# The normalised input h made straight from PSUM by ScalarE and VectorE, and the first loads in another order

## The chip, the cores and the metric

The kernel runs on one core of a Trainium2 chip. The metric is the device time of one execution, in microseconds, median of several runs.

## The reference

Two layers of an encoder over 256 positions and 2048 channels, all in f32. Cut to what matters here:

```
for l in range(2):
    h    = rms_norm(x, g_mix_pre[l])
    proj = h @ w_in[l]                     # 2048 -> 4096: q, k, v, and u for the pooling
    attn = dilated_mixture_attention(rope(q), rope(k), v)
    pool = multiscale_pool(u, w_pool[l], pool_scale[l])
    x    = x + rms_norm(concat(rms_norm(attn), rms_norm(pool)) @ w_out[l], g_mix_post[l])
    h2   = rms_norm(x, g_ffn_pre[l])
    f    = square(relu(h2 @ w_up[l])) @ w_down[l]        # 2048 -> 8192 -> 2048
    x    = x + rms_norm(f, g_ffn_post[l])
```

A product of two f32 matrices is made on TensorE as three products of rounded operands: every operand v is split into a high part (v rounded to the type fp32r) and a low part (v minus the high part), and hi*hi + lo*hi + hi*lo is summed in PSUM.

## The kernel before

**Units.** The work is cut into units: 512 output columns, all 2048 input channels, both row tiles t = 0, 1 of 128 positions. The weights of a unit are 8 pairs (two tiles of 128 channels by 512 columns, 512 KB). A pair goes through SyncE's DMA into one of 4 slots of `raw`, ScalarE casts it to `w_hi` (L692), VectorE subtracts and gets `w_lo` (L964), and TensorE uses it in 6 matmuls for t = 0 and in 6 more for t = 1 (`pair`, L377 to L379). `w_hi` and `w_lo` have 8 slots each; a slot is free again after its t = 1 matmuls (`w_used`), a `raw` slot after L964 (`lo_made`). `unit` runs n = 0 to 3: n = 0, 1 are the two halves of the input channels for t = 0, n = 2, 3 the same for t = 1; p = 0 to 3 are the pairs of a half. A place in a unit is written (n, p) below.

**The chunks of h.** h is needed transposed. It is 8 chunks: i = 4t + c is row tile t, channels 512c to 512c + 511. For each, TensorE transposes four blocks of x into `t_bank[i % 2]` (`h_turns`, L405); VectorE multiplies by the norm weight, which is one number per partition and block, and copies to `xg` in SBUF (`scaled`, L971); ScalarE casts that to `h_hi` (L697); GpSimd subtracts and gets `h_lo` (`stationary_lo`, L1297). `t_bank` is free for chunk i + 2 when `xg` of chunk i is made, `xg` when `h_lo` is made. The factor 1/rms of a row comes only with the result (L727). A matmul pair of the first unit on h waits for the chunk that holds its channels.

**Transitions.** h is made four times: at the start, in the middle of each layer (before the first unit with w_up), and between the layers. In these three transitions chunks 0 and 1 are transposed two pairs ahead of chunks 2 and 3, at the end of the product before; chunks 4, 5 are transposed at (1, 1) and chunks 6, 7 at (2, 1) of the first unit on h. x itself is renewed by VectorE (`add_posts`, L991) from the sum `acc`, GpSimd's product with the norm weight (L1324), and 1/rms, which GpSimd makes (L1316) from squares that ScalarE sums (L872, L713).

**What sets the order.** All of it is written out by hand: each engine runs its own list in order, and semaphores bind the lists. What stands behind a waiting instruction on its engine waits too. Loops over layers, groups and units are real loops on every engine.

## Time and profile before

| | us |
|---|---|
| median of 3 runs | 2080.79 (2079.71 to 2081.98) |
| span of the profiled execution | 2081.2 |
| TensorE busy, and share of the span | 2046.5, 98% |
| VectorE busy, share | 1088.2, 52% |
| ScalarE busy, share | 998.6, 48% |
| GpSimd busy, share | 212.1, 10% |

The span runs from the first to the last instruction of the core; it lies 0.4 us above the median and within the runs. No other time of the profiled execution is given, so the span stands for it. The page also has the granted clock of TensorE and the DMA traffic in 40 slices of the span; over the whole span 183 GB/s were moved.

### The profile page before, as it was taken

Reading aid. Unit: us, or ns where it says so; the run is one execution under the profiler, and the core shown is the slowest. Engines: PE = TensorE matmul, PEld = TensorE weight load, DVE = VectorE, ACT = ScalarE, POOL = GpSimd, SP = SyncE. Lnnn points to the kernel's source line nnn. Section 1 sums busy time; section 2 is a strip of 40 time slices with the busy share of each in tenths; the row PEclk is TensorE's granted clock in tenths of the full one; section 3 lists DMA queues with packets and bytes.
Section 4 is the critical chain, followed back from the end, with each engine's and each line's share of the span. In section 5 each row is a group of like instructions: output and inputs, shape, how many; then the busy total and the mean of one; then the engine's idle time right before and its main releaser. Section 6 shows DMA issues by size and latency. Waiting matters only on the chain.

```text
span 2081.2 us, 28816 instructions
## 1 busy us (share of the span) xinstructions
PE 2046.5 (98%) x9298; PEld 1695.0 (81%) x9298; DVE 1088.2 (52%) x1105; ACT 998.6 (48%) x1247; POOL 212.1 (10%) x248
## 2 busy tenths in 40 slices
PE   7999999999999999999989999999999999999998
PEld 5888887888888888888878888878888888888886
DVE  6554657554554554554554446664454454454454
ACT  5444656543553453454454446565345444444542
POOL 3951014000000000000120010230000000000001
PEclk9999999999999999999999999999999999999999
DMA  6664454565565555655556544555565566466463
GB/s 214 222 207 137 140 184 160 177 205 186 181 196 188 187 189 188 213 191 182 165 195 208 191 142 130 166 185 183 185 202 191 173 202 200 162 195 230 161 196 128
DMA packets 196518, 381.65 MB, mean 183 GB/s; under 512 B 11904, under 2 KB 14048, under 8 KB 195808
## 3 DMA queue, kind: packets, MB, share of 16 engines
q1 hardware_dynamic: 195776, 379.12, 55.7%
q10 hardware_dynamic: 672, 1.61, 0.2%
q8 instruction: 42, 0.69, 0.1%
q14 instruction: 28, 0.23, 0.0%
HBM read 378.59 MB, written 2.10 MB: 183 GB/s over the span
## 4 chain that ended last, share of the span: by engine, by line
PE 48%; issue 41%; POOL 8%; DMA 1%; DVE 0%; POOLq 0%; ACT 0%; SPq 0%; ACTq 0%; DVEq 0%
PE acc_bank L377 16%; PE acc_bank L379 16%; PE acc_bank L378 16%; POOL acc L1324 2%; POOL h_lo L1297 1%; PE t_bank L637 1%; POOL f_lo L1297 1%; DMA post_row<-in_g_ffn_post 1%; DMA x<-in_x 1%; POOL rstd L1316 0%; PE t_bank L405 0%; POOL band L1453 0%; POOL band L1447 0%; POOL tmp L1417 0%; POOL tmp L1423 0%
## 5 line engine op out<-in xcount | busy, mean ns | idle before, releaser
L964 DVE TENSOR_TENSOR w_lo<-raw,w_hi 128x1024 fp32r<-128x1024 f32 x704 | 871.5, 1250 | 573.4 <-ACT w_hi L692 538.9
L692 ACT CAST w_hi<-raw 128x1024 fp32r<-128x1024 f32 x704 | 734.1, 1052 | 481.7 <-PE acc_bank L379 265.9
L377 PE MATMUL acc_bank<-w_hi,h_hi 128*128 128x512 f32 x1536 | 608.9, 396 | 3.9 <-POOL h_lo L1297 2.2
L379 PE MATMUL acc_bank<-w_hi,h_lo 128*128 128x512 f32 x1536 | 600.0, 391 | 0.0
L378 PE MATMUL acc_bank<-w_lo,h_hi 128*128 128x512 f32 x1536 | 599.3, 390 | 0.0
L377 PE MATMUL acc_bank<-w_hi,f_hi 128*128 128x512 f32 x1216 | 477.4, 393 | 0.0
L379 PE MATMUL acc_bank<-w_hi,f_lo 128*128 128x512 f32 x1216 | 473.5, 389 | 0.0
L378 PE MATMUL acc_bank<-w_lo,f_hi 128*128 128x512 f32 x1216 | 473.1, 389 | 0.0
L377 PEld LDWEIGHTS acc_bank<-w_hi,h_hi 128*128 128x128 f32 x1536 | 289.8, 189 | 65.4 <-DVE w_lo L964 4.0
L379 PEld LDWEIGHTS acc_bank<-w_hi,h_lo 128*128 128x128 f32 x1536 | 289.0, 188 | 61.3
L378 PEld LDWEIGHTS acc_bank<-w_lo,h_hi 128*128 128x128 f32 x1536 | 289.7, 189 | 57.9
L379 PEld LDWEIGHTS acc_bank<-w_hi,f_lo 128*128 128x128 f32 x1216 | 228.2, 188 | 47.9
L378 PEld LDWEIGHTS acc_bank<-w_lo,f_hi 128*128 128x128 f32 x1216 | 228.4, 188 | 46.6
L377 PEld LDWEIGHTS acc_bank<-w_hi,f_hi 128*128 128x128 f32 x1216 | 228.3, 188 | 46.3
L1324 POOL TENSOR_TENSOR acc<-acc,post_row 128x512 f32<-128x512 f32 x32 | 43.2, 1353 | 1369.0 <-ACT junk L872 1369.0
L911 ACT CAST f_hi<-t_bank 128x512 f32 x64 | 37.6, 587 | 216.7 <-PE t_bank L637 216.7
L1221 DVE TENSOR_TENSOR f_lo<-t_bank,f_hi 128x512 f32 (+1 forms) x64 | 44.3, 692 | 186.0 <-ACT f_hi L911 186.0
L902 ACT ACTIVATE act_f<-acc_bank,rstd 128x512 f32<-128x512 f32 x64 | 43.8, 685 | 99.0 <-PE acc_bank L379 99.0
L1234 DVE TENSOR_TENSOR acc<-acc_bank,acc 128x512 f32 (+1 forms) x48 | 33.0, 688 | 99.2 <-PE acc_bank L379 99.2
L872 ACT ACTIVATE junk<-acc 128x512 f32<-128x512 f32 (+1 forms) x32 | 20.2, 632 | 93.0 <-DVE acc L1234 58.2
L1297 POOL TENSOR_TENSOR h_lo<-xg,h_hi 128x512 fp32r<-128x512 f32 x32 | 55.3, 1749 | 38.6 <-ACT h_hi L697 38.6
L1297 POOL TENSOR_TENSOR f_lo<-xg,f_hi 128x512 fp32r<-128x512 f32 x16 | 20.5, 1293 | 339.8 <-ACT f_hi L697 339.8
(150 smaller groups left out, 822.2 us busy)
## 6 DMA issues: line engine op xcount, KB each, us to landing
raw<-in_w_up SPq DMA_DIRECT2D x256, 512.0 KB, 4.4
raw<-in_w_down SPq DMA_DIRECT2D x256, 512.0 KB, 5.4
raw<-in_w_in SPq DMA_DIRECT2D x128, 512.0 KB, 4.8
raw<-in_w_out SPq DMA_DIRECT2D x64, 512.0 KB, 5.3
w_pool_s<-in_w_pool SPq DMA_DIRECT2D x2, 1024.0 KB, 8.5
post_row<-in_g_mix_post SPq DMA_DIRECT2D x2, 1024.0 KB, 7.3
post_row<-in_g_ffn_post SPq DMA_DIRECT2D x2, 1024.0 KB, 7.9
out<-x SPq DMA_DIRECT2D x8, 256.0 KB, 2.7
```

Source lines behind the costliest of these rows:

```text
L377: pe.matmul(bank[:, :], xh, wh, start=begin and k == 0, stop=False)
L378: pe.matmul(bank[:, :], xh, wl, start=False, stop=False)
L379: mm = pe.matmul(bank[:, :], xl, wh, start=False, stop=end and k == 1)
L637: tr = pe.transpose(t_bank[t][:, h_cols(j)], act_f[:, t, h_cols(j)], ident[:, :])
L692: act.copy(w_hi[:, half * PAIRS + p, :], raw[:, p, :]).then_inc(hi_made, 1)
L902: act.activation(act_f[:, t, :], acc_bank[t][:, :], ACT.Relu, scale=rstd[:, COL_X2 + t:COL_X2 + t + 1]).then_inc(acc_free[t], 1)
L911: act.copy(f_out(f_hi, u, t), t_bank[t][:, :].rearrange("p (k n) -> p k n", k=4)).then_inc(fhi_made, 1)
L964: dve.tensor_tensor(w_lo[:, slot, :], raw[:, p, :], w_hi[:, slot, :].bitcast(F32), ALU.subtract).then_inc(lo_made, 1)
L1221: dve.tensor_tensor(f_out(f_lo, u, t), t_bank[t][:, :].rearrange("p (k n) -> p k n", k=4), f_out(f_hi, u, t).bitcast(F32), ALU.subtract).t ...
L1234: dve.tensor_tensor(dst, acc_bank[t][:, :], dst, ALU.add).then_inc(acc_free[t], 1)
L1297: pool.tensor_tensor(lo, xg[:, slot, :].rearrange("p (k n) -> p k n", k=k), hi.bitcast(F32), ALU.subtract).then_inc(st_lo, 1)
L1324: pool.tensor_tensor(part, part, post_row[:, c_cols(c)], ALU.mult).then_inc(post_ready, 1)
```

## The change

1. **h without a copy.** ScalarE makes `h_hi` straight from `t_bank` in PSUM: four instructions of 128x128 for a chunk, each with its norm weight as per-partition scale (`h_hi_pair`). VectorE makes `h_lo` from `t_bank`, the norm weight and `h_hi`: four instructions of 128x128 (t_bank times gain minus h_hi). L971, L697 and L1297 go for the 32 chunks of h (the y and attention chunks keep them), and GpSimd has no part in h.
2. **Waits.** VectorE waits for all of a chunk's `h_hi`. TensorE's transposes of chunk i >= 2 wait for `h_lo` of chunk i - 2, where they waited for `xg` of chunk i - 2. TensorE's matmuls wait for half chunks.
3. **First loads.** The norm weights and the second half of x's first row tile are issued first by ScalarE, without a wait; SyncE issues the first half, four weight pairs, the second row tile, the small inputs, and then goes on with weights.
4. **The start.** VectorE makes no zeros in `acc` and does not add them to x. Chunks 2 and 3 are transposed within the first unit, before (0, 1) and (0, 2), and the other norm weights before (1, 3). The lists of ScalarE and VectorE mix chunks and weight pairs in another order.

The diff, with some of the like pieces left out:

```diff
                 with sp.Fori(0, CHUNKS) as c:
                     load_unit(w_down, l, g * D, c * CH, hu + 2 * CHUNKS + c * 2)
+            load_half(w_in, 0, 0, 3 * HALF_W, 0)
+            sp.dma_start(x[:, 1, :], x_rows[1]).then_inc(x_loaded[2], 16)
+            row = 0
+            for g in (g_ffn_pre, g_attn_out, g_pool_out):
+                n = DEPTH * g.shape[1] // P
+                sp.dma_start(rows_others[row:row + n, :], g.rearrange("l (k p) -> (l k) p", p=P)
+                             ).then_inc(others_loaded, 16)
+                row += n
+            sp.dma_start(pos_i[:, :], positions[0].rearrange("(t p) -> p t", p=P),
+                         allow_slow_non_contiguous=True).then_inc(pos_loaded, 16)
             with sp.Fori(0, DEPTH) as l:
                 hu = l * HU_LAYER
-                with sp.Fori(0, 2) as u:
-                    load_unit(w_in, l, 0, 3 * HALF_W + u * CH, hu + u * 2)
+                with sp.If(l > 0):
+                    load_half(w_in, l, 0, 3 * HALF_W, hu)
+                load_half(w_in, l, HALF_W, 3 * HALF_W, hu + 1)
+                load_unit(w_in, l, 0, 3 * HALF_W + CH, hu + 2)
                 sp.wait_ge(acc_done, l * ACC_LAYER + 1)
...
                     pe.wait_ge(x_ready, l * 16 + 8 * h + i + 1)
                     if i >= 2:
-                        pe.wait_ge(xg_ready, l * XG_LAYER + (0, XG_H2)[h] + i - 1)
+                        pe.wait_ge(h_lo_made, h_pair(l, h, i - 1))
                     for j in range(4):
                         tr = pe.transpose(t_bank[i % 2][:, h_cols(j)],
                                           x[:, t, c * CH + j * P:c * CH + (j + 1) * P],
...
                         h_turns(l, h, (4, 5))
                     if (n, p) == (2, 1):
                         h_turns(l, h, (6, 7))
-                    if p % 2 == 0:
-                        pe.wait_ge(st_lo, XG_SLOTS + l * XG_LAYER + (0, XG_H2)[h]
-                                   + 2 * n + p // 2 + 1)
+                    pe.wait_ge(h_lo_made, h_pair(l, h, 2 * n + p // 2) + p % 2 + 1)
                 return before
...
                          ).then_inc(gains_turned, 1)
             h_turns(0, 0, (0, 1))
-            pe.wait_ge(others_loaded, 16 * 3)
-            pe.transpose(s_bank[1][:, 0:4 * KT], rows_others[:, :], ident[0:4 * KT, 0:4 * KT]
-                         ).then_inc(gains_turned, 1)
-            h_turns(0, 0, (2, 3))
+            def others_turn():
+                pe.wait_ge(others_loaded, 16 * 3)
+                pe.transpose(s_bank[1][:, 0:4 * KT], rows_others[:, :], ident[0:4 * KT, 0:4 * KT]
+                             ).then_inc(gains_turned, 1)
             with pe.Fori(0, DEPTH) as l:
                 hu0 = l * HU_LAYER
                 a0 = l * ACC_LAYER
                 xg0 = XG_SLOTS + l * XG_LAYER
-                unit(hu0, a0, h_hi, h_lo, h_first_unit(l, 0))
+                h_before = h_first_unit(l, 0)
+                def first_before(n, p):
+                    if (n, p) in ((0, 1), (0, 2)):
+                        with pe.If(l < 1):
+                            h_turns(0, 0, (p + 1,))
+                    if (n, p) == (1, 3):
+                        with pe.If(l < 1):
+                            others_turn()
+                    h_before(n, p)
+                unit(hu0, a0, h_hi, h_lo, first_before)
                 with pe.Fori(1, 6) as u:
                     unit(hu0 + u * 2, a0 + u, h_hi, h_lo)
...
                     act.wait_ge(w_used, hu * PAIRS + p + 1)
                     act.copy(w_hi[:, half * PAIRS + p, :], raw[:, p, :]).then_inc(hi_made, 1)
+            def h_hi_pair(bank, g, dst):
+                for n in range(2):
+                    for j in (2 * n, 2 * n + 1):
+                        hi = act.mul(dst[:, j, :], bank[:, h_cols(j)],
+                                     gain[:, g + j:g + j + 1])
+                    hi.then_inc(h_hi_made, 1)
             def stationary_hi(i, dst, slot, k):
...
             def h_chunks(l, h, which):
                 for i in which:
                     t, c = i // CHUNKS, i % CHUNKS
-                    stationary_hi(l * XG_LAYER + (0, XG_H2)[h] + i,
-                                  h_hi[:, 4 * c:4 * c + 4, h_cols(t)], i % 2, 4)
+                    act.wait_ge(tb_done[i % 2], l * TB_LAYER + (0, TB_H2)[h] + i // 2 + 1)
+                    h_hi_pair(t_bank[i % 2], (G_MIX, G_FFN)[h] + 4 * c,
+                              h_hi[:, 4 * c:4 * c + 4, h_cols(t)])
             def h_squares(l, h, t):
...
+            x_rows = x_in[0].rearrange("(t p) d -> t p d", p=P)
+            act.dma_start(rows_mix[:, :], g_mix_pre.rearrange("l (k p) -> (l k) p", p=P)
+                          ).then_inc(gains_loaded, 16)
+            act.dma_start(x[:, 0, D // 2:], x_rows[0][:, D // 2:]).then_inc(x_loaded[1], 16)
             act.wait_ge(ones_made, 1)
             act.copy(warm[:, :], ones[:, :]).then_inc(warm_done, 1)
-            x_rows = x_in[0].rearrange("(t p) d -> t p d", p=P)
-            act.wait_ge(x_loaded[0], 16)
-            row = 0
-            for g in (g_ffn_pre, g_attn_out, g_pool_out):
-                n = DEPTH * g.shape[1] // P
-                act.dma_start(rows_others[row:row + n, :], g.rearrange("l (k p) -> (l k) p", p=P)
-                              ).then_inc(others_loaded, 16)
-                row += n
-            act.dma_start(x[:, 0, D // 2:], x_rows[0][:, D // 2:]).then_inc(x_loaded[1], 16)
-            act.dma_start(pos_i[:, :], positions[0].rearrange("(t p) -> p t", p=P),
-                          allow_slow_non_contiguous=True).then_inc(pos_loaded, 16)
+            act.wait_ge(gain_ready, 1)
+            h_chunks(0, 0, (0,))
             split_hi(0, 0, (0,))
-            act.dma_start(x[:, 1, :], x_rows[1]).then_inc(x_loaded[2], 16)
-            h_chunks(0, 0, (0, 1))
-            split_hi(0, 0, (1, 2))
-            h_chunks(0, 0, (2, 3))
-            split_hi(0, 0, (3,))
+            h_chunks(0, 0, (1,))
+            split_hi(0, 0, (1, 2, 3))
+            h_chunks(0, 0, (2,))
             split_hi(1, 1, (0,))
+            h_chunks(0, 0, (3,))
             with act.Fori(0, DEPTH) as l:
                 hu0 = l * HU_LAYER
...
                 mix_square(0, 2)
                 mix_square(0, 3)
                 split_hi(hu_f, 0)
+                act.wait_ge(gain_ready, 4 + 2 * l)
                 h_chunks(l, 1, (0, 1))
...
             def h_chunks(l, h, which):
                 for i in which:
-                    dve.wait_ge(tb_done[i % 2], l * TB_LAYER + (0, TB_H2)[h] + i // 2 + 1)
-                    scaled(l * XG_LAYER + (0, XG_H2)[h] + i, i % 2, t_bank[i % 2],
-                           (G_MIX, G_FFN)[h] + 4 * (i % CHUNKS), 4)
+                    t, c = i // CHUNKS, i % CHUNKS
+                    g = (G_MIX, G_FFN)[h] + 4 * c
+                    for n in range(2):
+                        dve.wait_ge(h_hi_made, h_pair(l, h, i) + 2)
+                        for j in (2 * n, 2 * n + 1):
+                            lo = dve.scalar_tensor_tensor(
+                                h_lo[:, 4 * c + j, h_cols(t)], t_bank[i % 2][:, h_cols(j)],
+                                gain[:, g + j:g + j + 1],
+                                h_hi[:, 4 * c + j, h_cols(t)].bitcast(F32),
+                                ALU.mult, ALU.subtract)
+                        lo.then_inc(h_lo_made, 1)
...
-            def h_first_unit(l, h, hu):
-                add_posts(l, h, (4, 5))
+            def h_first_unit(l, h, hu, late=True):
+                if late:
+                    add_posts(l, h, (4, 5))
                 split_lo(hu + 1, 1, (2, 3))
...
             dve.wait_ge(x_loaded[0], 16)
             dve.sem_inc(x_ready, 2)
             dve.wait_ge(gain_ready, 1)
-            h_chunks(0, 0, (0, 1))
-            split_lo(0, 0, (0, 1))
             dve.wait_ge(x_loaded[1], 16)
             dve.sem_inc(x_ready, 2)
-            h_chunks(0, 0, (2, 3))
-            split_lo(0, 0, (2, 3))
+            h_chunks(0, 0, (0,))
+            split_lo(0, 0, (0,))
+            h_chunks(0, 0, (1,))
+            split_lo(0, 0, (1, 2, 3))
+            h_chunks(0, 0, (2,))
+            split_lo(1, 1, (0,))
+            h_chunks(0, 0, (3,))
+            split_lo(1, 1, (1,))
+            dve.wait_ge(x_loaded[2], 16)
+            dve.sem_inc(x_ready, 4)
+            h_first_unit(0, 0, 0, False)
             dve.wait_ge(gains_turned, 2)
             half = KT // 2
             for at_col, n, src in ((G_FFN, KT, 0), (G_ATTN, half, 2 * KT), (G_POOL, half, 3 * KT)):
...
                 src = s_bank[1][:, (2 + n) * KT:(3 + n) * KT]
                 dve.tensor_copy(gains_half[:, n, 0:DEPTH, :],
                                 src.rearrange("p (l k) -> p l k", l=DEPTH)).then_inc(gains_ready, 1)
-            split_lo(1, 1, (0, 1))
             dve.wait_ge(gain_ready, 4)
             dve.wait_ge(gains_ready, 4)
-            dve.wait_ge(setup_done, 4)
...
                 pool.tensor_tensor(lo, xg[:, slot, :].rearrange("p (k n) -> p k n", k=k),
                                    hi.bitcast(F32), ALU.subtract).then_inc(st_lo, 1)
-            def h_chunks(l, h, which):
-                for i in which:
-                    t, c = i // CHUNKS, i % CHUNKS
-                    stationary_lo(l * XG_LAYER + (0, XG_H2)[h] + i,
-                                  h_hi[:, 4 * c:4 * c + 4, h_cols(t)],
-                                  h_lo[:, 4 * c:4 * c + 4, h_cols(t)], i % 2, 4)
             def h_first_unit(l, h):
                 root(l, (RS_X1, RS_X2)[h], (COL_X1, COL_X2)[h])
-                h_chunks(l, h, range(4, 8))
                 root(l, (RS_X1, RS_X2)[h] + 1, (COL_X1, COL_X2)[h] + 1)
```

## Where the instructions stand

The rows name the line, the operation, output <- inputs and what is waited for. First TensorE at the start of the program, before:

```order
L430 MATMUL s_bank<-ident,rows_mix 128x32 [waits gains_loaded,ident_made]
L405 MATMUL t_bank<-ident,x 128x128 [waits x_ready]
L405 MATMUL t_bank<-ident,x 128x128 x3
L405 MATMUL t_bank<-ident,x 128x128 [waits x_ready]
L405 MATMUL t_bank<-ident,x 128x128 x3
L434 MATMUL s_bank<-ident,rows_others 128x64 [waits others_loaded]
L405 MATMUL t_bank<-ident,x 128x128 [waits xg_ready,x_ready]
L405 MATMUL t_bank<-ident,x 128x128 x3
```

And in the change, up to the first matmuls of the first pair and the transposes of chunk 2 (L420 is now the line of the transposes, L392 to L394 are the pair's):

```order
L443 MATMUL s_bank<-ident,rows_mix 128x32 [waits gains_loaded,ident_made]
L420 MATMUL t_bank<-ident,x 128x128 [waits x_ready]
L420 MATMUL t_bank<-ident,x 128x128 x3
L420 MATMUL t_bank<-ident,x 128x128 [waits x_ready]
L420 MATMUL t_bank<-ident,x 128x128 x3
...
L392 MATMUL acc_bank<-w_hi,h_hi 128x512 [waits lo_made]
L393 MATMUL acc_bank<-w_lo,h_hi 128x512
L394 MATMUL acc_bank<-w_hi,h_lo 128x512
...
L420 MATMUL t_bank<-ident,x 128x128 [waits h_lo_made,x_ready]
L420 MATMUL t_bank<-ident,x 128x128 x3
```

The product with the other norm weights and chunks 2 and 3 stood ahead of the first pair, and now stand behind or within it.

Second, VectorE in the middle of a layer, from the end of the four instructions on x, before:

```order
L991 SCALAR_TENSOR_TENSOR x<-acc,rstd,x 128x512 [waits post_ready]
...
L971 TENSOR_TENSOR xg<-t_bank,gain 128x512 [waits st_lo]
L970 REGISTER_ALU [waits tb_done1]
L971 TENSOR_TENSOR xg<-t_bank,gain 128x512 [waits st_lo]
...
L964 TENSOR_TENSOR w_lo<-raw,w_hi 128x1024 [waits hi_made]
...
L1179 SCALAR_TENSOR_TENSOR acc<-acc_bank,rstd,acc 128x512 [waits w_used]
```

And in the change (L1020 is the line on x, L1031 makes h_lo, L993 w_lo, L1223 is L1179 before):

```order
L1020 SCALAR_TENSOR_TENSOR x<-acc,rstd,x 128x512 [waits post_ready]
...
L1031 SCALAR_TENSOR_TENSOR h_lo<-t_bank,gain,h_hi 128x128 [waits h_hi_made]
L1031 SCALAR_TENSOR_TENSOR h_lo<-t_bank,gain,h_hi 128x128
...
L993 TENSOR_TENSOR w_lo<-raw,w_hi 128x1024 [waits hi_made]
...
L1223 SCALAR_TENSOR_TENSOR acc<-acc_bank,rstd,acc 128x512 [waits w_used]
```

The place in VectorE's list is the same, but what stood there waited for TensorE (`tb_done`) and GpSimd (`st_lo`), and now waits for ScalarE (`h_hi_made`).

Third, ScalarE at the same place, in the change (L716 casts w_hi, L722 makes h_hi, L899 sums squares of acc):

```order
L716 CAST w_hi<-raw 128x1024 [waits w_used]
L917 ISA
L722 ACTIVATE h_hi<-t_bank,gain 128x128 [waits tb_done0,gain_ready]
L722 ACTIVATE h_hi<-t_bank,gain 128x128 x3
L722 ACTIVATE h_hi<-t_bank,gain 128x128 [waits tb_done1]
L722 ACTIVATE h_hi<-t_bank,gain 128x128 x3
L898 REGISTER_ALU [waits acc_free1]
L899 ACTIVATE junk,ss_post<-acc 128x512 [waits sq_done]
L722 ACTIVATE h_hi<-t_bank,gain 128x128 [waits tb_done0]
```

The eight instructions of chunks 0 and 1 stand where two casts from `xg` stood: behind the last of four weight casts, and chunks 2 and 3 stay behind the squares.

## Rows read from the trace of the kernel before

**Rows 1.** The page: busy time of each engine, share of the span, instructions
```profile
PE 2046.5 (98%) x9298; PEld 1695.0 (81%) x9298; DVE 1088.2 (52%) x1105; ACT 998.6 (48%) x1247; POOL 212.1 (10%) x248
```

**Rows 2.** Waits of TensorE: us in total, times, longest
```profile
PE t_bank L405 <- DVE x L991: 10.0, 6, 4.6
```

**Rows 3.** Timeline, start: start us, us, engine, line, tiles, [idle before <-releaser]
```profile
5.87 1.97 PE L405 MATMUL t_bank<-ident,x 128*128 128x128 f32 x8 [3.03 <-DVEq L1030]
...
7.16 0.44 ACTq L748 DMA_DIRECT2D x<-in_x  x1
...
8.32 1.04 ACT L692 CAST w_hi<-raw 128x1024 fp32r<-128x1024 f32 x1 [6.02 <-DMA raw<-in_w_in]
...
13.88 1.97 PE L405 MATMUL t_bank<-ident,x 128*128 128x128 f32 x8 [1.96 <-DVEq L1035]
...
15.50 0.78 PE L377 MATMUL acc_bank<-w_hi,h_hi 128*128 128x512 f32 x1
```

**Rows 4.** DMA, the first 60 us in 40 slices of 1.5 us
```profile
GB/s 0 104 233 309 366 407 356 339 376 391 408 218 22 165 212 300 156 362 335 305 242 22 11 0 11 0 0 0 35 302 305 247 307 328 374 400 379 395 389 341
```

**Rows 5.** Timeline: end of the first unit, and the second
```profile
32.12 0.50 PE L377 MATMUL acc_bank<-w_hi,h_hi 128*128 128x512 f32 x1 [2.16 <-POOL h_lo L1297]
...
34.43 0.47 PE L377 MATMUL acc_bank<-w_hi,h_hi 128*128 128x512 f32 x1
...
39.67 3.88 ACT L692 CAST w_hi<-raw 128x1024 fp32r<-128x1024 f32 x4
...
54.36 0.50 PE L377 MATMUL acc_bank<-w_hi,h_hi 128*128 128x512 f32 x1 [0.20 <-DVE w_lo L964]
```

**Rows 6.** Timeline of the first mid-layer transition, TensorE, ScalarE, VectorE
```profile
317.23 3.48 DVE L964 TENSOR_TENSOR w_lo<-raw,w_hi 128x1024 fp32r<-128x1024 f32 x3
...
317.87 1.14 ACT L697 CAST h_hi<-xg 128x512 fp32r<-128x512 f32 x2
...
318.08 1.03 PE L405 MATMUL t_bank<-ident,x 128*128 128x128 f32 x8
...
330.71 2.32 DVE L991 SCALAR_TENSOR_TENSOR x<-acc,rstd,x 128x512 f32<-128x512 f32 x2 [0.54 <-POOL rstd L1316]
...
332.43 1.97 PE L405 MATMUL t_bank<-ident,x 128*128 128x128 f32 x8 [2.40 <-DVE x L991]
...
334.05 0.78 PE L377 MATMUL acc_bank<-w_hi,h_hi 128*128 128x512 f32 x1
```

**Rows 7.** Windows around it: us, busy time of each engine, granted clock (PEclk), DMA
```profile
331.00:336.00 5.00, 3.57 (x13) 3.21 (x14) 5.00 (x8) 2.43 (x8) 1.36 (x2) 0.66 0.50 146
```

**Rows 8.** Timeline of the transition between the layers, ScalarE and TensorE
```profile
1037.24 1.05 ACT L692 CAST w_hi<-raw 128x1024 fp32r<-128x1024 f32 x1 [1.82 <-PE acc_bank L379]
...
1046.70 0.63 ACT L872 ACTIVATE junk<-acc 128x512 f32<-128x512 f32 x1 [0.94 <-DVE acc L1234]
...
1050.95 2.94 ACT L692 CAST w_hi<-raw 128x1024 fp32r<-128x1024 f32 x3 [3.53 <-issue]
...
1056.06 1.97 PE L405 MATMUL t_bank<-ident,x 128*128 128x128 f32 x8 [4.61 <-DVE x L991]
```

**Rows 9.** Groups of instructions by form: busy us, mean ns of one, idle before
```profile
L692 ACT CAST w_hi<-raw 128x1024 fp32r<-128x1024 f32 x704 | 734.1, 1052 | 481.7 <-PE acc_bank L379 265.9 <-DMA raw<-in_w_down 114.6 <-DMA raw<-in_w_in 59.1
...
L697 ACT CAST h_hi<-xg 128x512 fp32r<-128x512 f32 x32 | 19.3, 620 | 36.7 <-DVE xg L971 36.7
...
L727 ACT ACTIVATE proj<-acc_bank,rstd 128x512 f32<-128x512 f32 x12 | 8.2, 681 | 6.6 <-PE acc_bank L379 6.6
...
L964 DVE TENSOR_TENSOR w_lo<-raw,w_hi 128x1024 fp32r<-128x1024 f32 x704 | 871.5, 1250 | 573.4 <-ACT w_hi L692 538.9
...
L971 DVE TENSOR_TENSOR xg<-t_bank,gain 128x512 f32<-128x512 f32 x40 | 26.2, 685 | 30.1 <-PE t_bank L405 14.1 <-PE t_bank L487 12.0 <-POOL h_lo L1297 3.9
...
L1179 DVE SCALAR_TENSOR_TENSOR acc<-acc_bank,rstd,acc 128x512 f32<-128x512 f32 x8 | 6.0, 745 | 1.8 <-POOL rstd L1316 1.8
...
L1297 POOL TENSOR_TENSOR h_lo<-xg,h_hi 128x512 fp32r<-128x512 f32 x32 | 55.3, 1749 | 38.6 <-ACT h_hi L697 38.6
```

26 lines of the change are left out of this document (12 added, 14 removed).

## The prediction

> **What bounds the kernel now.** I read the page first: TensorE is busy 2046.5 of 2081.2 us [rows 1]. None of its matmuls goes away, so the change can only reach the 34.7 us in which TensorE idles, and all of the change lies at four places: the start and three transitions. The waits of TensorE say where idling is dearest: 10.0 us for the new x (L991) [rows 2]. Then I read timelines at those places.
>
> At the start, the reader is to see a queue of loads behind waits. The second half of x's first row tile is issued only at 7.16, and TensorE turns it at 13.88; the first matmul of the product comes at 15.50 [rows 3]. It idles again for 2.16 until 32.12, for GpSimd's h_lo [rows 5].
>
> In the middle of a layer the two rows to look at are 318.08 and 332.43 [rows 6]. At 318.08 chunks 2 and 3 are transposed with no wait, because VectorE has emptied `t_bank` early. At 332.43 TensorE has waited 2.40 us for x: that is the end of a chain of VectorE and ScalarE steps, not of TensorE's. The granted clock is 0.66 in 331 to 336 [rows 7], so this is in part at the lower level of 1.2 GHz; eight transposes take 1.97 there and 1.03 at 318.08. Between the layers the same chain ends at 1056.06 after a wait of 4.61 [rows 8].
>
> **Prices of the new instructions.** No row has a 128x128 ScalarE instruction on PSUM, so I bound it. 512 more columns cost ScalarE 1052 - 620 = 432 ns (L692, L697), 0.84 ns a column; L727, from PSUM with a per-partition scale, takes 681 ns [rows 9]; 384 columns less gives 0.36 us. Four casts in a row took 3.88 where four alone are 4.21 [rows 5], an overlap of 0.11. So a chunk costs a = 4 x 0.36 - 3 x 0.11 = 1.1; I take 1.15 to the start of VectorE. VectorE: (1250 - 685)/512 = 1.1 ns a column, L1179 is 745 ns [rows 9], less 0.42 gives 0.32 us; three L964 in 3.48 [rows 6] show an overlap of at least 0.1. d = 4 x 0.32 - 3 x 0.1 = 1.0, with the handover 1.1. Bounds: below, no more than the wide instructions replaced, a = 0.62 and d = 0.69; above, no overlap, a = 1.45 and d = 1.28.
>
> Here a rule speaks against the change. The row: a chunk cost VectorE 0.69 and ScalarE 0.62 in one instruction each [rows 9], and the sums above make that 1.0 and 1.1 in four. The Trainium skill, page "VectorE: DVE Perf Modes", section on the TRN2 errata, advises tiles of 512 elements or more since a fixed cost is paid per instruction. The Trainium skill, page "ScalarE: Activation LUTs", section "What ACT_TABLE_LOAD costs", gives 280 + 0.833 N ns with one pointer operand and 93 ns of overlap, an estimate of 1.27 for the chunk; by that the result would be about 1 us later than mine.
>
> **The start: -6.2 us.** Both halves of x's first row tile are now issued at about 1.3. Adding the slices (rate times 1.5 us), 1.5 MB had come by 7.5 us and 2.1 MB by 9 [rows 4]; x's two halves and the first weight pair are 1.5 MB with parts of the next pairs between, so that pair is there at about 8.5, like now (8.32 [rows 3]). Chunk 0 is turned by 6.8, h_hi by 8.0, h_lo by 9.2, all under that load. Cast 1.05 and w_lo 1.25 [rows 9]: the first matmul at 10.9, not 15.5. From there to (2, 1), which stands at 34.43 [rows 5]: nine pairs of 1.37 (14 pairs from 34.43 to 54.36 are 1.42 each with their small waits [rows 5]) are 12.4, six chunks of transposes 2.4, the slow first pair 1.2 more, the small product 0.1. Waits left: h_lo of chunks 4 and 5, behind VectorE's last two w_lo, ScalarE's four squares and a + d: about 0.9. Sum 27.9, 6.5 earlier than 34.43. The loads beyond the first four pairs queue behind 4 MB that are in by 14.2 at these rates, and each comes about 0.5 us before its need. In the second unit TensorE waited for w_lo, DMA behind it; the cushion between the casts of 39.67 and that unit's start shrinks by 0.4, so 0.3 of the gain goes. The zeros and x additions left out are cover gained, nothing on the path. Bounds: -7.5 if the waits vanish; -4.5 if loads come 2 us late.
>
> **Middle of a layer: +2.5 us each, twice.** Chunk 0's transposes are long done, but ScalarE is in the weight casts until 317.87 [rows 6] (the last waits for TensorE), and its h work stands behind them. Before, VectorE had emptied `t_bank` by then, without ScalarE. Now: chunk 0 h_hi 319.0, h_lo 320.1; chunk 1 h_lo 321.3. TensorE, at 318.08 ready for chunks 2 and 3, waits for both: about 2.0 and then 0.8. That is a new stall of 3 us, yet it is not the price, since TensorE then waited for x anyway. The price is read from VectorE's list behind it. Its three w_lo began at 317.23 and now begin at 321.3: 324.8. Then in order: sum of block (1, 2) 0.7; ScalarE's square, which waits for that, 0.7; chunks 2 and 3 on ScalarE, behind the square in its list, 2.3; h_lo 1.1; w_lo 1.2; sum 0.7; w_lo 1.2; the mean and w_lo 1.4 plus the cast it waits for, 0.5; x 0.7. The end is 335.3; before, the first x came shortly ahead of 332.43. What is saved there is in this sum: GpSimd's four 1.75 [rows 9] are out, and the two x instructions take 0.7 each instead of 2.32 for both [rows 6].
>
> That saving has a rule beside it: the Trainium skill, page "SBUF — State Buffer", section "Who interferes with whom", says a VectorE instruction with two SBUF inputs contends with a GpSimd one that reads SBUF; the 2.32 against twice 0.7 agrees.
>
> TensorE gets to this place at 334.3 and waits only 1.1, so its clock need not fall; the matmuls begin at 336.5. Before they began at 334.05 [rows 6] at the lower clock, worth 334.8 at the full one. That is +1.7. Then chunks 6 and 7: their x is queued behind h_lo of 4 and 5, which now waits for ScalarE's squares and a: +0.8. Total 2.5. With the low prices the chain is 2.9 shorter (4 a and 2 d): -0.4, as a gain. With the high ones, and the clock falling at the new stalls, +4.2.
>
> **Between the layers: +2.4 us.** ScalarE is free at 1038.2 [rows 8]. Then 2a + d to 1041.6, three w_lo 1045.1, chunks 2 and 3 on VectorE 1047.2 (ScalarE's part is hidden behind the w_lo), w_lo 1048.4, sum 1049.1. Before, the square that follows stood at 1046.70 [rows 8]. All behind it is as before: ScalarE's 3.53 us without a cause in the trace ahead of 1050.95, cast, w_lo, loop, x. So +2.4; the wait of 4.61 hides the early stall. The added branches on VectorE and TensorE are counted as nothing, hidden by that wait; the one at (1, 3) isn't hidden, 0 to 0.3. Bounds 0 to +3.6.
>
> **Sum.** -6.2 + 2.5 + 2.5 + 2.4 = +1.2 on a span of 2081.2, which is 0.4 above the median: 2082.0.
>
> **Rivals.**
> - The forecast: start and transitions about cancel. 2082.0, from 2079 to 2085. Chance 0.52.
> - Short instructions are cheap. If a and d are near the lower bounds, the chain between the layers and those within cost -0.4, -0.4 and 0, and the start gives -6.7: 2073.5; half way, 2076. For it: nothing in the rows has this form, and TensorE's stall at 318.08 would be below 1.5. Against it: L727 has 0.68 for 512 columns, whose fixed part can't be below 0.25. Chance 0.17.
> - Slower by new waits, my other side. TensorE waits for h_lo at chunks 2 and 3 in all three transitions; an idle of 2.16 left the clock up [rows 5], one of 2.40 was followed by slow transposes [rows 6], and the new one is about 2.0 and 0.8. If the clock falls there, and a and d are at the upper end so that the later waits are no cover, each transition costs 4: +12 - 6 = 2086.8. It decides from a + d above 2.5 on. Chance 0.22.
> - The start gives little, because the loads come later than the slices say (x's second row tile, 1 MB, and the small inputs now stand on SyncE's queue ahead of the second half's weights): -3 instead of -6.2, 2085.2. Chance 0.09.
>
> **How the numbers follow.** The time is the forecast's. The range reaches to halfway of the cheap case and to the slow one: 2075.5 to 2087.5. A measurement can tell 0.2%, 4.2 us: faster means below 2076.6, slower above 2085.0. Faster: 0.17. Slower: 0.22 and half of the last, 0.26. Within: 0.57.
>
> **What would show it.** In the profile after: the first matmul of the product at 10.9; (2, 1) of the first unit near 28; the new L1031 near 0.32 and L722 near 0.36 us; a wait of TensorE's transposes (L420) for h_lo of about 2 us where 318.08 stands, less the start's gain; the matmuls behind the next transposes (334.05 now) at 330.3, that is 336.5 less 6.2; L993 below L964's 1250. Wrong would be: no such wait; ScalarE's work on h starting before the last weight cast; or a first unit held by DMA waits.

## The result, and the profile after

The changed kernel takes 2085.05 us (median of 16 runs, 2083.24 to 2087.55), the kernel before beside it 2081.69 (16 runs, 2079.71 to 2083.57). The ratio is 1.0017, with a 95% interval of 1.0011 to 1.0024. So it is slower by 3.4 us, 0.17%: certain in sign, and by the ratio inside the 0.2% that the prediction called no change. In microseconds the prediction drew that line at 2085.0, from three runs of the kernel before; 2085.05 lies 0.05 beyond it, and sixteen runs put the kernel before 0.9 higher.

The spans of every run are known now, and they correct one reading. A run's time is its span plus 1.7 to 1.8 us (1.9 to 2.1 in the last two kernels below). The profiled execution of before, with its span of 2081.2, was therefore one of 2083.0, 1.3 above its kernel's median: the median span of before is 2079.6 (27 runs) to 2080.4 (21 runs). The profiled execution of after has 2083.1, 0.2 below its median. In spans of the two profiles the change costs 1.9 us, in medians 3.4.

The page of after, busy times [rows 1]; under it the waits of TensorE (us in total, times, longest) [rows 2]:

```profile
PE 2049.3 (98%) x9298; PEld 1696.4 (81%) x9298; DVE 1084.1 (52%) x1196; ACT 1012.2 (49%) x1343; POOL 150.4 (7%) x216
...
PE t_bank L420 <- DVE x L1020: 9.3, 6, 5.0
PE t_bank L420 <- DVE h_lo L1031: 6.7, 5, 2.0
...
PE acc_bank L392 <- DVE w_lo L993: 3.3, 3, 2.9
```

The wait for x is nearly what it was (10.0), though the start's waits are down. The line for h_lo is new: 6.7 us, the five waits of chunks 2 and 3 in the three transitions. TensorE is also busy 2.8 us longer with the same 9298 matmuls.

**The start.** Timeline of after [rows 3, 5] (start us, us, engine, line, tiles, idle before and its releaser):

```profile
7.76 1.04 ACT L716 CAST w_hi<-raw 128x1024 fp32r<-128x1024 f32 x1 [0.17 <-DMA raw<-in_w_in]
...
10.11 0.79 PE L392 MATMUL acc_bank<-w_hi,h_hi 128*128 128x512 f32 x1 [2.92 <-DVE w_lo L993]
...
14.78 0.40 PE L392 MATMUL acc_bank<-w_hi,h_hi 128*128 128x512 f32 x1
...
27.21 1.03 PE L420 MATMUL t_bank<-ident,x 128*128 128x128 f32 x8
28.00 0.47 PE L392 MATMUL acc_bank<-w_hi,h_hi 128*128 128x512 f32 x1
```

The product begins at 10.11 (15.50 before), and the matmul of (2, 1) stands at 28.00 (34.43 before): 6.43 us earlier.

**Middle of a layer.** Timeline of after, first mid-layer transition [rows 6]:

```profile
307.59 1.32 PE L420 MATMUL t_bank<-ident,x 128*128 128x128 f32 x8 [0.23 <-DVE x L1020]
...
310.32 1.05 ACT L716 CAST w_hi<-raw 128x1024 fp32r<-128x1024 f32 x1 [1.88 <-PE acc_bank L394]
311.27 2.16 ACT L722 ACTIVATE h_hi<-t_bank,gain 128x128 fp32r<-128x128 f32 x8
...
313.62 0.66 PE L420 MATMUL t_bank<-ident,x 128*128 128x128 f32 x4 [1.98 <-DVE h_lo L1031]
...
314.51 3.48 DVE L993 TENSOR_TENSOR w_lo<-raw,w_hi 128x1024 fp32r<-128x1024 f32 x3
...
314.65 0.91 PE L420 MATMUL t_bank<-ident,x 128*128 128x128 f32 x4 [0.38 <-DVE h_lo L1031]
...
318.77 0.63 ACT L899 ACTIVATE junk<-acc 128x512 f32<-128x512 f32 x1 [5.34 <-DVE acc L1223]
...
320.56 2.16 DVE L1031 SCALAR_TENSOR_TENSOR h_lo<-t_bank,gain,h_hi 128x128 fp32r<-128x128 f32 x8 [1.90 <-ACT h_hi L722]
...
326.32 2.35 POOL L1360 TENSOR_TENSOR acc<-acc,post_row 128x512 f32<-128x512 f32 x1
...
327.46 2.43 DVE L1020 SCALAR_TENSOR_TENSOR x<-acc,rstd,x 128x512 f32<-128x512 f32 x2
...
329.36 1.31 PE L420 MATMUL t_bank<-ident,x 128*128 128x128 f32 x8 [1.53 <-DVE x L1020]
...
335.98 1.03 PE L420 MATMUL t_bank<-ident,x 128*128 128x128 f32 x8
```

Where chunks 2 and 3 were turned without a wait (318.08 in [rows 6]) TensorE now waits 1.98 and 0.38 for h_lo. ScalarE's work on chunks 0 and 1 begins at 311.27, behind four weight casts, though their transposes were done by 308.9; ahead of the fourth cast it stood 1.88 us for TensorE. ScalarE then idles 5.34 us ahead of the square at 318.77, with chunks 2 and 3 behind it in its list.

**Between the layers, and the second mid-layer transition** [rows 8]:

```profile
1044.29 0.63 ACT L899 ACTIVATE junk<-acc 128x512 f32<-128x512 f32 x1 [0.75 <-DVE acc L1278]
...
1048.81 2.94 ACT L716 CAST w_hi<-raw 128x1024 fp32r<-128x1024 f32 x3 [3.80 <-issue]
...
1054.11 1.97 PE L420 MATMUL t_bank<-ident,x 128*128 128x128 f32 x8 [5.00 <-DVE x L1020]
...
1349.12 2.15 PE L420 MATMUL t_bank<-ident,x 128*128 128x128 f32 x8 [1.98 <-DVE h_lo L1031]
...
1364.99 1.31 PE L420 MATMUL t_bank<-ident,x 128*128 128x128 f32 x8 [2.10 <-DVE x L1020]
```

**A ledger.** I measure each transition from the transposes of chunks 0, 1 over those of 4, 5 to those of 6, 7 (their start times in the traces), and the start by the transposes of chunks 6, 7:

| us | before | after | differs |
|---|---|---|---|
| start, to chunks 6, 7 | 33.64 | 27.21 | -6.43 |
| first middle: to 4, 5 / on to 6, 7 | 18.26 / 7.91 | 21.77 / 6.62 | +3.51 / -1.29 |
| between the layers | 21.56 / 7.94 | 24.15 / 8.74 | +2.59 / +0.80 |
| second middle | 18.24 / 8.00 | 21.92 / 8.22 | +3.68 / +0.22 |

The sum is +3.1; the rest of the program runs 1.2 us shorter, in pieces of 0.15 to 0.64 that I did not trace to a cause. Together this is the 1.9 between the spans.

The second halves show what sets them. Windows from 4, 5 to 6, 7, of after and then of before [rows 7] (us; busy time of PE, PEld, DVE, ACT, POOL; granted clock, DMA share, GB/s):

```profile
1054.11:1062.85 8.74, 8.74 (x32) 7.30 (x33) 6.27 (x15) 2.70 (x10) 0.54 (x1) 0.72 0.43 127
329.36:335.98 6.62, 6.61 (x32) 5.38 (x33) 6.16 (x15) 4.23 (x15) 0.54 (x1) 1.00 0.78 239
1364.99:1373.21 8.22, 8.21 (x32) 6.50 (x33) 6.35 (x15) 4.23 (x14) 0.54 (x1) 0.79 0.62 194
```

```profile
1056.06:1064.00 7.94, 7.94 (x32) 6.73 (x33) 6.52 (x9) 1.94 (x4) 3.91 (x3) 0.80 0.48 146
332.43:340.34 7.91, 7.91 (x33) 6.73 (x33) 6.51 (x9) 2.29 (x6) 3.92 (x3) 0.80 0.53 185
```

TensorE is busy in all of each stretch. The work is the same, and they go by the granted clock: 6.62 at 1.00, 7.9 at 0.80, 8.2 at 0.79, 8.74 at 0.72. Where the level of 1.2 GHz (0.50) lies in after, two more windows show:

```profile
315.00:318.00 3.00, 3.00 (x10) 2.43 (x9) 3.00 (x4) 0.00 (x0) 0.00 (x0) 0.50 0.28 51
...
1349.50:1352.00 2.50, 2.50 (x11) 1.99 (x10) 2.50 (x5) 0.00 (x0) 0.00 (x0) 0.50 0.00 0
```

In the first middle the clock fell once, behind the h_lo wait instead of the x wait. In the second it fell twice, behind the h_lo wait at 1349 and again at 1366.2. Between the layers it was low from 1052.2 to 1059.0; before, from 1055.8 to 1059.2. Counted from the start of the transposes that is 4.9 us against 3.2, at half speed worth 0.9, and +0.80 is there. A fall ahead of a wait for x costs little, since TensorE would have waited anyway; behind the wait it costs about half its length.

### The profile page after: what moved, and what is told of

Read it like the earlier page. It is cut to its first block, busy times and chain, and to the rows that moved or that the text cites. A ratio compares the mean times of both kernels' runs of the same rounds, so it can differ in the third digit from the quotient of the medians.

```text
span 2083.1 us, 28880 instructions
## 1 busy us (share of the span) xinstructions
PE 2049.3 (98%) x9298; PEld 1696.4 (81%) x9298; DVE 1084.1 (52%) x1196; ACT 1012.2 (49%) x1343; POOL 150.4 (7%) x216
## 4 chain that ended last, share of the span: by engine, by line
PE 49%; issue 42%; POOL 6%; DVE 1%; DMA 1%; ACT 0%; POOLq 0%; DVEq 0%; SPq 0%; ACTq 0%
PE acc_bank L394 16%; PE acc_bank L392 16%; PE acc_bank L393 16%; POOL acc L1360 2%; PE t_bank L661 1%; POOL f_lo L1341 1%; DMA post_row<-in_g_ffn_post 1%; DVE w_lo L993 1%; DVE x L1020 0%; PE t_bank L420 0%; DVE h_lo L1031 0%; POOL rstd L1352 0%; POOL tmp L1459 0%; POOL band L1489 0%; POOL band L1483 0%
## 5 line engine op out<-in xcount | busy, mean ns | idle before, releaser
L993 DVE TENSOR_TENSOR w_lo<-raw,w_hi 128x1024 fp32r<-128x1024 f32 x704 | 862.8, 1239 | 561.1 <-ACT w_hi L716 527.2
L716 ACT CAST w_hi<-raw 128x1024 fp32r<-128x1024 f32 x704 | 733.0, 1052 | 469.3 <-PE acc_bank L394 263.3
L392 PE MATMUL acc_bank<-w_hi,h_hi 128*128 128x512 f32 x1536 | 609.2, 397 | 3.6 <-DVE w_lo L993 3.3
L394 PE MATMUL acc_bank<-w_hi,h_lo 128*128 128x512 f32 x1536 | 600.4, 391 | 0.0
L392 PE MATMUL acc_bank<-w_hi,f_hi 128*128 128x512 f32 x1216 | 477.3, 393 | 0.0
L394 PE MATMUL acc_bank<-w_hi,f_lo 128*128 128x512 f32 x1216 | 473.4, 389 | 0.0
L392 PEld LDWEIGHTS acc_bank<-w_hi,h_hi 128*128 128x128 f32 x1536 | 289.7, 189 | 64.0 <-DVE w_lo L993 5.1
L394 PEld LDWEIGHTS acc_bank<-w_hi,h_lo 128*128 128x128 f32 x1536 | 289.5, 188 | 61.6
L394 PEld LDWEIGHTS acc_bank<-w_hi,f_lo 128*128 128x128 f32 x1216 | 228.3, 188 | 47.7
L392 PEld LDWEIGHTS acc_bank<-w_hi,f_hi 128*128 128x128 f32 x1216 | 228.4, 188 | 46.4
L1360 POOL TENSOR_TENSOR acc<-acc,post_row 128x512 f32<-128x512 f32 x32 | 42.3, 1325 | 1394.0 <-ACT junk L899 1394.0
L899 ACT ACTIVATE junk<-acc 128x512 f32<-128x512 f32 (+1 forms) x32 | 20.2, 632 | 102.7 <-DVE acc L1278 58.1
L760 ACT ACTIVATE proj<-acc_bank,rstd 128x512 f32 (+1 forms) x32 | 21.9, 684 | 66.3 <-PE acc_bank L394 66.3
L1031 DVE SCALAR_TENSOR_TENSOR h_lo<-t_bank,gain,h_hi 128x128 fp32r<-128x128 f32 x128 | 34.7, 342 | 28.8 <-ACT h_hi L722 28.8
```

The source lines that it names most:

```text
L392: pe.matmul(bank[:, :], xh, wh, start=begin and k == 0, stop=False)
L394: mm = pe.matmul(bank[:, :], xl, wh, start=False, stop=end and k == 1)
L716: act.copy(w_hi[:, half * PAIRS + p, :], raw[:, p, :]).then_inc(hi_made, 1)
L760: act.mul(proj_out(u, t), acc_bank[t][:, :], rstd[:, COL_X1 + t:COL_X1 + t + 1]).then_inc(acc_free[t], 1)
L993: dve.tensor_tensor(w_lo[:, slot, :], raw[:, p, :], w_hi[:, slot, :].bitcast(F32), ALU.subtract).then_inc(lo_made, 1)
L1031: lo = dve.scalar_tensor_tensor(h_lo[:, 4 * c + j, h_cols(t)], t_bank[i % 2][:, h_cols(j)], gain[:, g + j:g + j + 1], h_hi[:, 4 * c + j, h ...
```

## The experiments

Each time is the median of 5 or 11 runs, with the kernel before timed on the same chip. The load order alone, the old middles and the two kernels with ScalarE's chunks earlier shared one chip (before: 2081.32), the other four another (2082.11). Segment lengths are those of the ledger.

### Only the load order

The kernel before, with part 3 of the change alone; chunks, waits and GpSimd's work as before.

```diff
+            load_half(w_in, 0, 0, 3 * HALF_W, 0)
+            sp.dma_start(x[:, 1, :], x_rows[1]).then_inc(x_loaded[2], 16)
+            row = 0
+            for g in (g_ffn_pre, g_attn_out, g_pool_out):
...
+            act.dma_start(rows_mix[:, :], g_mix_pre.rearrange("l (k p) -> (l k) p", p=P)
+                          ).then_inc(gains_loaded, 16)
+            act.dma_start(x[:, 0, D // 2:], x_rows[0][:, D // 2:]).then_inc(x_loaded[1], 16)
```

> The kernel before with part 3 of the change alone: the first loads in the new order and on the new queues, h still by xg and GpSimd, the engines' lists otherwise as before. It tells what share of the start's 6.4 us comes from the loads. Theory A (loads and the path of h both count): x's second half lands near 6.5 instead of 13.8, but VectorE and ScalarE still make chunks 0 and 1 and chunks 2 and 3 before the first pair can go, and GpSimd needs 1.75 us a chunk: first matmul of the product near 11.5, (2, 1) of the first unit near 30.5, time 3.5 to 4.5 us below before (ratio 0.998). Rival B (loads alone): (2, 1) at 28, time 6 below. Rival C (the path of h alone): less than 1.5 us below.

Measured: 2084.04, ratio 1.0014 (1.0005 to 1.0023). It is slower, which no theory had expected. The timeline of its start:

```profile
15.26 0.37 PE L445 MATMUL s_bank<-ident,rows_others 64*128 64x64 f32 x1 [7.87 <-DMA rows_others<-in_g_pool_out]
15.55 1.97 PE L416 MATMUL t_bank<-ident,x 128*128 128x128 f32 x8
...
33.85 0.80 PE L388 MATMUL acc_bank<-w_hi,h_hi 128*128 128x512 f32 x1 [2.21 <-POOL h_lo L1300]
```

TensorE's list has the small product of the other norm weights ahead of chunks 2 and 3, and its rows now load behind four weight pairs and x. So TensorE stands 7.87 us, and chunks 6, 7 are turned at 36.58 instead of 33.64. Here one 64x64 product in front of the chunks holds the start, and the next experiment takes it away.

### The load order, and that product moved

As above, with the small product at (1, 3) of the first unit, as part 4 of the change has it, and VectorE's use of it behind the chunks.

```diff
             h_turns(0, 0, (0, 1))
-            pe.wait_ge(others_loaded, 16 * 3)
-            pe.transpose(s_bank[1][:, 0:4 * KT], rows_others[:, :], ident[0:4 * KT, 0:4 * KT]
-                         ).then_inc(gains_turned, 1)
             h_turns(0, 0, (2, 3))
...
+                    if (n, p) == (1, 3):
+                        with pe.If(l < 1):
+                            others_turn()
```

> As e1_loads_only, but TensorE's small product with the other norm weights stands inside the first unit, ahead of (1, 3), and VectorE's copies of it behind the first unit's work on h; h by xg and GpSimd as before. In e1 TensorE waited 7.9 us for that product's rows, which now load behind 3.5 MB, with chunks 2 and 3 and the first pair queued behind it. Theory G (that wait alone made e1 slow): first matmul of the product at 11 to 12 instead of 16.9, transposes of chunks 6 and 7 in the first unit at 30 to 31 (33.6 before), time 2.5 to 4 us below before. Rival H (the loads in the new order are slower in themselves, whatever waits for them): first matmul later than 14, time at or above before.

Measured: 2080.28, ratio 0.9993 (0.9984 to 1.0002): 1.8 us below the kernel before, where the last one was 2.7 above. The interval of the ratio reaches 1, so the gain over the kernel before isn't certain, but the 3.8 between the two kernels is. Theory G has the cause; its numbers were too good (12.56 for 11 to 12, 31.41 for 30 to 31, 1.8 for 2.5 to 4). Timeline of its start:

```profile
10.94 1.97 PE L416 MATMUL t_bank<-ident,x 128*128 128x128 f32 x8 [3.70 <-DVEq L1048]
12.56 0.78 PE L388 MATMUL acc_bank<-w_hi,h_hi 128*128 128x512 f32 x1
...
29.92 0.50 PE L388 MATMUL acc_bank<-w_hi,h_hi 128*128 128x512 f32 x1 [2.83 <-POOL h_lo L1312]
...
31.41 1.03 PE L416 MATMUL t_bank<-ident,x 128*128 128x128 f32 x8
```

Chunks 6, 7 are turned 2.2 us earlier than before, and the median falls by 1.8. Of the start's 6.43 us this is 2.2; the other 4.2 need parts 1 and 4 together (chunks 2, 3 inside the unit; h_lo of 4, 5 without GpSimd, whose wait of 2.83 here is 0.2 in the change). The runs do not split these. The first row shows one piece of it: the second half of x is issued at 1.27 and lands 6.1 us later, but TensorE waits for it until 10.94, since VectorE passes on that x is there (`x_ready`) only behind two w_lo in its list. Part 4 moved that ahead of them.

### The middle of a layer as before

The change, but the mid-layer chunks go through `xg` and GpSimd again. One piece of the edit; the lists of ScalarE, VectorE and GpSimd go back in the same way.

```diff
-                        pe.wait_ge(h_lo_made, h_pair(l, h, i - 1))
+                        if h:
+                            pe.wait_ge(xg_ready, l * XG_LAYER + XG_H2 + i - 1)
+                        else:
+                            pe.wait_ge(h_lo_made, h_pair(l, h, i - 1))
```

> The change with one part undone: in the middle of both layers h goes by xg and GpSimd again, in the place in each list that it had before; the start and the transition between the layers stay as in the change. Theory A (each mid-layer transition costs 2.2 us, and 3.9 where the clock falls): both prices go, the start's 6.4 us and the 2.7 us between the layers stay, so about 2081.7 - 6.4 + 2.7 = 2078.0, 3.7 below before and some 6 to 7 below the change; in the trace the transposes of chunks 6 and 7 in the middle of the first layer come 26.2 us after those of chunks 0 and 1, as before (28.4 in the change). Rival D (the loss is not in the transitions but comes from elsewhere, such as another code layout or traffic): the time stays at the change's.

Measured: 2079.77, ratio 0.9994 (0.9985 to 1.0003); span 2077.4, 5.7 below after. The middles take 26.40 and 25.75 again (before 26.17, 26.24; after 28.39, 30.14), a difference of 6.4. That the middles cost more than the change lost in all is shown. Between the layers, left as in the change, it takes 31.63 (32.89 after), with a wait for x of 3.14 instead of 5.00. Two things differ there in the traces. ScalarE's idle without a cause is 3.03 for 3.80, so x comes 0.8 sooner. And the clock fell behind the h_lo wait of 1.96 (0.50 in 1037.5 to 1040.5), so TensorE came later to the place where it waits for x. So a part of that term varies with no edit there. The time was to be 2078.0 by theory A and is 1.8 above.

### ScalarE's chunks one cast earlier

The change; ScalarE does chunks 0 and 1 ahead of its fourth weight cast, the one that waits for TensorE, in all three transitions.

```diff
-                split_hi(hu_f, 0)
+                split_hi(hu_f, 0, (0, 1, 2))
                 act.wait_ge(gain_ready, 4 + 2 * l)
                 h_chunks(l, 1, (0, 1))
+                split_hi(hu_f, 0, (3,))
```

The same move is made between the layers.

> The change, with ScalarE's chunks 0 and 1 of h moved ahead of the fourth weight cast in all three transitions, into the 1.9 us in which ScalarE waits for TensorE there. Nothing is taken away, the instructions are the same. Theory A (the price is the place of ScalarE's work: VectorE and TensorE wait for it): chunk 1's h_lo is ready 2 us earlier, TensorE's wait for h_lo ahead of chunks 2 and 3 falls from 2.0 and 0.4 to below 0.5, each transition gets 1.5 to 2.5 us shorter, total 2085 - 6 = 2079, 2 to 3 below before. Rival E (the price is the number and length of the short instructions): the time stays within 1 us of the change's 2085, since they are all still there.

Measured: 2076.68, ratio 0.9979 (0.997 to 0.9988). Timeline of its first middle:

```profile
309.15 2.17 ACT L722 ACTIVATE h_hi<-t_bank,gain 128x128 fp32r<-128x128 f32 x8
...
312.32 1.03 PE L420 MATMUL t_bank<-ident,x 128*128 128x128 f32 x8
...
321.79 0.50 PE L392 MATMUL acc_bank<-w_hi,h_hi 128*128 128x512 f32 x1 [0.27 <-DVE w_lo L995]
...
327.37 1.53 PE L420 MATMUL t_bank<-ident,x 128*128 128x128 f32 x8 [2.13 <-DVE x L1022]
```

ScalarE begins at 309.15, right behind the transposes, and chunks 2 and 3 are turned at 312.32 with no wait. The time is 8.4 below the change, where 6 was expected. So one cast's place in a list is enough to bring the wait for h_lo or to take it away, with the short instructions all still there; what their length adds, the wide kernel below shows. The middles take 27.21 each: the wait for x is still 2.13, and the low clock is back behind it.

### Chunks 2 and 3 ahead of the square

On top of that, in the middles, ScalarE does chunks 2 and 3 before the square that it idled 5.34 us for.

```diff
                 split_hi(hu_f, 0, (3,))
-                mix_square(1, 2)
                 h_chunks(l, 1, (2, 3))
+                mix_square(1, 2)
```

> As e3_act_early, and in the middle of the layers ScalarE's chunks 2 and 3 moved ahead of the square that waits for VectorE (L899). Theory A: in the change ScalarE idles 5.3 us ahead of that square, and VectorE then 1.9 us for h_hi of chunks 2 and 3; with the work in the idle time VectorE's list ends 1.5 to 2 us earlier in both mid-layer transitions, so 3 us below e3, near 2076, 5 to 6 below before. Rival E: as e3. Rival F (after e3 the transition is bound by TensorE or by the weight casts, not by this list): no more than 1 us below e3.

Measured: 2071.70, ratio 0.9955 (0.9942 to 0.9969), 5.0 below the last kernel where 3 was expected. The middles take 23.66 and 23.64, 2.5 less than the kernel before. Windows of 45 us around the three transitions (granted clock third from the end):

```profile
300.00:345.00 45.00, 43.59 (x208) 35.51 (x207) 32.88 (x64) 30.59 (x70) 7.54 (x9) 1.00 0.41 130
1025.00:1070.00 45.00, 39.52 (x179) 32.59 (x179) 29.18 (x60) 26.70 (x63) 2.89 (x4) 0.92 0.41 129
1335.00:1380.00 45.00, 43.59 (x210) 35.49 (x209) 35.87 (x65) 33.25 (x73) 4.46 (x6) 1.00 0.50 163
```

The x wait is 1.16 in the middles, and the clock doesn't fall there. Each middle gained 3.6 on the last kernel, 2.0 up to chunks 4, 5 and 1.6 behind. Of the 2.0, 1.0 is the wait for x, and most of the rest are short waits of TensorE for w_lo (321.79 in the last timeline, and another at 323.58), which are gone. The 1.6 is the clock: from 4, 5 to 6, 7 it was 0.79 in the last kernel and is 1.00 here, with TensorE busy throughout in both. Between the layers x is still waited for 5.31.

### One wide instruction for four short ones

The change with one 128x512 instruction for a chunk on each of the two engines. It takes the norm weight of the first block for all four blocks; only the time is read from it.

```diff
-                for n in range(2):
-                    for j in (2 * n, 2 * n + 1):
-                        hi = act.mul(dst[:, j, :], bank[:, h_cols(j)], gain[:, g + j:g + j + 1])
-                    hi.then_inc(h_hi_made, 1)
+                act.mul(dst, bank[:, :].rearrange("p (k n) -> p k n", k=4),
+                        gain[:, g:g + 1]).then_inc(h_hi_made, 2)
```

> The change with one instruction of 128x512 for a chunk on ScalarE and one on VectorE instead of four of 128x128 each; all four blocks of a chunk are scaled with the norm weight of the first, so that part of the computation is changed. It measures the price of the short instructions by itself, with every place in the lists as in the change. By the change's rows four take 1.14 and 1.12 us, 1.0 and 1.04 from chunk to chunk; one wide one should take 0.69 and 0.75. Theory A counts 4 a + 2 d in a mid-layer transition and 2 a + 3 d between the layers: 2.4 and 2.0 us shorter, about 6 in all, 2079. Rival I (only the place of ScalarE's work counts): less than 2 us below the change.

Measured: 2077.53, ratio 0.9978 (0.9969 to 0.9987), 7.5 us less than the change (both as medians beside their own kernel before: 7.9). Groups by form, of after and then of this kernel (count, busy us, mean ns):

```profile
L722 ACT ACTIVATE h_hi<-t_bank,gain 128x128 fp32r<-128x128 f32 x128 | 34.9, 379 | 21.1 <-PE t_bank L420 21.1
L1031 DVE SCALAR_TENSOR_TENSOR h_lo<-t_bank,gain,h_hi 128x128 fp32r<-128x128 f32 x128 | 34.7, 342 | 28.8 <-ACT h_hi L722 28.8
```

```profile
L1026 DVE SCALAR_TENSOR_TENSOR h_lo<-t_bank,gain,h_hi 128x512 fp32r<-128x512 f32 x32 | 22.7, 746 | 25.9 <-ACT h_hi L720 23.0 <-DMA x<-in_x 2.8
L720 ACT ACTIVATE h_hi<-t_bank,gain 128x512 fp32r<-128x512 f32 x32 | 20.5, 680 | 22.7 <-PE t_bank L420 22.7
```

A chunk takes 0.68 instead of 1.14 on ScalarE and 0.75 instead of 1.12 on VectorE. The h_lo wait falls to 1.22, no clock falls in the middles, and they take 26.3 each; between the layers it is 29.6 (32.9 in after). Theory A, which counted the chunk's new prices alone, had 6. So length and place both count, each by itself for more than the change lost: they meet in the same waits, and their gains can't be added. The Trainium skill, page "VectorE: DVE Perf Modes", section on the TRN2 errata, says to use tiles of 512 or more. By this run that is worth 0.37 us a chunk on VectorE and 0.46 on ScalarE, and 7.5 on the kernel.

### The cast moved ahead of the loop's edge

The two-step reordering above, and one more weight cast ahead of the place where ScalarE idles between the layers ([rows 8]: 3.53 without a cause in the trace). At the start and in the middles the same cast is written at another place of the code, but ScalarE's order stays.

```diff
-                split_hi(hu + 1, 1, (1, 2, 3))
+                split_hi(hu + 1, 1, (2, 3))
...
+                    with act.If(l < DEPTH - 1):
+                        split_hi(hu + HU_GROUP + 1, 1, (1,))
```

> e4_act_early2 with one cast moved: ScalarE casts the second weight pair of the first unit's upper half ahead of its jump back to the head of the layer loop instead of behind it. In e4 VectorE waits 4.3 us for that cast (ScalarE spends 3.6 us at the loop's edge before it), then passes its own edge in 2.2 us, and only then renews x, for which TensorE waits 5.3 us. Theory J (the two edges stand one after the other, by that one wait): they now run side by side, x comes 3 to 4 us earlier between the layers, TensorE's wait falls from 5.3 to below 2.5, and the time is 3 us below e4's 2071.7, near 2068.7. Rival K (the cast is bound by its weights' DMA, or VectorE's edge gets longer): less than 1 us.

Measured: 2069.00, ratio 0.9934 (0.9921 to 0.9948). Timeline between the layers, first of the last kernel, then of this one:

```profile
1040.98 2.94 ACT L716 CAST w_hi<-raw 128x1024 fp32r<-128x1024 f32 x3 [3.58 <-issue]
1042.06 1.23 DVE L995 TENSOR_TENSOR w_lo<-raw,w_hi 128x1024 fp32r<-128x1024 f32 x1 [4.29 <-ACT w_hi L716]
...
1046.42 1.96 PE L420 MATMUL t_bank<-ident,x 128*128 128x128 f32 x8 [5.31 <-DVE x L1022]
```

```profile
1043.84 1.99 ACT L716 CAST w_hi<-raw 128x1024 fp32r<-128x1024 f32 x2 [3.51 <-issue]
1044.51 1.41 DVE L1026 SCALAR_TENSOR_TENSOR x<-acc,rstd,x 128x512 f32<-128x512 f32 x2 [2.69 <-issue]
1045.40 1.31 PE L420 MATMUL t_bank<-ident,x 128*128 128x128 f32 x8 [3.12 <-DVE x L1026]
```

ScalarE's idle of 3.5 is still there, now ahead of the next cast: it belongs to the place in the code, where the loop over the layers begins anew, and not to the cast. But VectorE's w_lo and x no longer stand behind it. From 0, 1 to 4, 5 it takes 19.1, where it took 21.2. The wait for x was to fall below 2.5 and is 3.12, since VectorE still waits 1.50 for a cast and then spends 2.69 at its own edge. The time is 2.7 below the last kernel's, which ran on the other chip; with each beside its own kernel before, it is 3.5.

### Two more moves

Besides, VectorE makes the sum of the last block ahead of its fourth w_lo, and both engines do chunks 4 and 5 ahead of ScalarE's squares and VectorE's mean.

```diff
                 h_chunks(l, 1, (2, 3))
-                split_lo(hu_f, 0, (3,))
                 mixed(1, 3)
+                split_lo(hu_f, 0, (3,))
...
                 split_hi(hu + 1, 1, (2, 3))
+                h_chunks(l, h, (4, 5))
                 h_squares(l, h, 0)
-                h_chunks(l, h, range(4, 8))
+                h_chunks(l, h, (6, 7))
```

> e7_edge and two more moves, nothing taken away: VectorE takes the last block of the product (mixed (1, 3), and between the layers the last sum) ahead of the fourth w_lo, and in the first unit chunks 4 and 5 stand ahead of the four squares on ScalarE and of the mean on VectorE, so that x of chunks 6 and 7 comes sooner. Theory A: the chain to the new x is 1.1 us shorter in each transition, as far as TensorE still waits there (1.2 in the middle of a layer), and the waits of 0.4 to 0.9 ahead of (2, 0) and (2, 1) go: 1.5 us in each of three transitions, 4 us below e7. Rival L (after e7 TensorE is nearly never waiting at these places, so nothing is left to gain): less than 1 us below e7.

Measured: 2067.30 (2065.03 to 2068.24), ratio 0.993 (0.9916 to 0.9943), mean clock 0.999. The medians fell by 1.7, less than expected; the profiled spans, one execution each, by 4.2. The row between the layers:

```profile
1042.35 1.31 PE L420 MATMUL t_bank<-ident,x 128*128 128x128 f32 x8 [1.39 <-DVE x L1027]
```

In its profiled run no transition has the low clock any more, and they take 23.4, 23.9 and 23.3 (before 26.2, 29.5, 26.2; the last kernel 23.7, 27.3, 23.6). So most of the gain in the profile lies between the layers, and in the middles, with 0.3 each, rival L is right. This is the fastest kernel here: 14.8 us below the one before, 0.7%. Its interval overlaps that of the last kernel.

## Why the prediction was right, and where its terms were off

The forecast was 2082.0 within 2075.5 to 2087.5, no change; 2085.05 came. The places and the mechanism were those: a start that gives 6 us, and three transitions that take it back, since VectorE and TensorE now wait for ScalarE's work on h. The size is less good, and "no change" was in part luck: +1.2 was forecast and +3.4 measured, the time lies just outside the 2079 to 2085 that the forecast gave itself among the rivals, and it is nearer to the slow rival's 2086.8 than to 2082.0.

**The prices.** a = 1.15 to the start of VectorE and d = 1.1 were predicted, with 0.36 and 0.32 for one instruction. The rows above show 0.379 and 0.342, a chunk 1.14 and 1.12. The Trainium skill, page "ScalarE: Activation LUTs", section "What ACT_TABLE_LOAD costs", gives a formula, by which this form is an estimate of 387 ns; the row's 379 is nearer to that than my 0.36. By its overlap of 93 ns the chunk would take 1.27; the row shows 1.14, so the overlap is 0.13 here.

**The start.** (2, 1) stands at 28.00 where 27.9 was said, 6.43 earlier for 6.5. The 0.3 that was to go in the second unit did not show: from 6, 7 to the first middle the program runs 0.15 shorter. Two errors cancel in the 27.9. The first weight pair was there at 7.76, not 8.5, so the product began at 10.11, not 10.9. Then the step "the slow first pair, 1.2 more" was too small: the matmuls were 0.43 apart until 14.5 and 0.23 apart only from there on, which takes in the first pair, the transposes of chunk 2 and half of the second pair. In the trace of before the slow work ends at 18.2, but transposes from 13.88 on had taken the first part of it [rows 3]; here the product itself has all of it.

**The middles.** +2.5 each was predicted; +2.2 and +3.9 came.
- The new stall was said to be "about 2.0 and then 0.8": 1.98 and 0.38. VectorE's three w_lo, said to begin at 321.3, less 6.6 for the earlier clock of events 314.7, began at 314.51. The chain up to there held.
- "The two x instructions take 0.7 each" failed in the first middle: they took 2.43. GpSimd's product L1360 runs from 326.32 to 328.67 beside the first x instruction (1.76 us, the other 0.74). I had put the old 2.32 down to GpSimd's work on h, and it is the product with the norm weight that still stands there. In the second middle L1360 was through at 1363.1, ahead of the x at 1364.11, and two x take 1.40. This bears out the Trainium skill, page "SBUF — State Buffer", section "Who interferes with whom", on the contention, and not my guess which GpSimd instruction it was.
- "TensorE gets to this place at 334.3" has a gap. Before, it got there at 330.03 (332.43 less 2.40), and the stalls of 2.8 make 332.8; nothing in the prediction accounts for the other 1.5. TensorE did come at 327.83, which is 334.4 by the clock of events of before, but by the stalls of 2.36 and by the clock that fell behind them, worth 1.7 (0.50 in 314.9 to 318.3). So the forecast wait of 1.1 (1.53 measured), and the matmuls at 330.43 for 330.3, came out by a fall that the forecast said need not happen.
- "Then chunks 6 and 7: +0.8" didn't happen. TensorE has no wait at 335.98, 1062.85 or 1373.21. TensorE is busy from chunks 4, 5 to 6, 7 in every transition. So for the first middle +3.0 up to 4, 5 and -0.5 behind were forecast, and +3.51 and -1.29 came.
- "Its clock need not fall" held for the x wait of the first middle (1.53; window at 1.00), but the clock had fallen at the h_lo stall instead. In the second middle it fell at both. That is the difference between +2.2 and +3.9, and it is what the slower rival said of the clock. I had taken it as all or nothing with a + d above 2.5, at 4 us a transition. With a + d = 2.26 the clock fell behind the new stall in two transitions of three, and one of them cost 3.9. So the point from which that rival was to decide was wrong, while its mechanism was at work in part.

**Between the layers.** +2.4 predicted, +3.4 came. Up to chunks 4, 5 it is +2.59: the square was to be 2.4 later than before and is 2.1 later (1046.70 less 4.54 is 1042.16, measured 1044.29), ScalarE's idle is 3.80 for 3.53. The other 0.80 is the clock: low for 4.9 us behind the transposes where it was low for 3.2. I had no term for the clock here.

**From the sum to the time.** The span of after should have been 2082.4, and is 2083.1. The other 2.35 of the miss are in "which is 0.4 above the median". A time is its span plus 1.7 to 1.8, so the profiled run of before took 2083.0 and was 1.3 above its kernel's median, while that of after took 2084.9, 0.2 below its own. To come from the span to the measured time 1.95 had to be added, and I took 0.4 off. Seen in medians, the base was 0.9 too low and the change's price 2.2 too low (+3.4 for +1.2). The profile of before also had the clock fall in both middles behind its waits of 2.4; the profile with the load order alone had it in neither behind the same waits, and there the stretch from 4, 5 to 6, 7 takes 7.50 for 7.9. Whether that is the 1.3 by which the profiled run lay above the median isn't shown.

**The other rivals.** Cheap short instructions: no, by the row of 379 and 342 ns, and the wide kernel shows what they would have been worth. Loads that come late: not in the change, whose first pair was there at 7.76. But the kernel with the load order alone shows how near it was. There the small product stays ahead of chunks 2 and 3, and the start loses 2.9 us. I had counted its place at (1, 3) as a branch of 0 to 0.3 and not seen that the start rests on it.

## What to carry to other kernels

When an edit hands a step from one engine to another, look where the step then stands in the new engine's list: here a cast and a square in front of it cost more than the shortness of its instructions (moving the work ahead of them gave 13.3 us, wide instructions 7.5), and a loss of 3.4 us became a gain of 9.6. When loads are put in another order, go through every instruction that waits for one that is now later, however small, and see what stands behind it. Price an idle of TensorE by its wait and by the granted clock in the stretch behind it, and take the base of a sum from several runs, not from the one that was profiled.

## What the runs showed of the hardware

- Idle and clock, over the ten traces and leaving out the first 20 us. No low level follows TensorE's waits of 1.03 to 1.53. From 1.96 to 2.83 it goes either way: in ten cases it follows (behind 1.96, 1.98, 2.10, 2.13, 2.21, 2.38 and 2.40, some more than once, at once or up to 1.3 us later), in ten it doesn't (1.96, 2.10, 2.16, 2.40, 2.41, 2.83). The same 2.40 was followed by it in the first middle of the kernel with the old middles and not in its second, nor in either middle of the kernel with the load order and the product moved. Behind the nine waits of 3.12 to 5.31, or within them, it came. So runs of one kernel differ by it: of the 16 of after, the four with a mean clock of 0.996 have spans of 2082.2 on average, the eight with 0.994 have 2084.0.
- At the start the matmuls are slow while the clock column says otherwise. A window of after:

```profile
10.00:12.50 2.50, 2.39 (x6) 1.90 (x7) 2.50 (x7) 2.42 (x3) 0.00 (x0) 1.00 1.07 424
```

Its matmuls start 0.43 us apart, as in 315 to 318 at 0.50. So the reading 1.00 says nothing of the matmuls' pace there.
- The edge of the layer loop idles ScalarE for 2.9 to 3.8 us and VectorE for 1.9 to 2.7, in the nine traces that show it without another cause. It is not a fixed price: with no edit there, ScalarE's idle is 3.80 in after and 3.03 in the kernel with the old middles.
- VectorE beside GpSimd: the instruction on x (128x512, two inputs in SBUF) takes 1.64 to 1.78 us where a GpSimd instruction on 512 columns is already running when it starts (75 cases in the ten traces), and 0.73 to 0.75 in all the others, also in the fourteen where such an instruction begins only after it.
